# Nine of the eleven input slots of each attention layer as seven block products

## What is computed

```python
for l in range(DEPTH):                      # DEPTH = 2
    h = rmsnorm(x, attn_norm[l])            # [256, 1024]
    proj = h @ w_in[l]                      # q_a, kv_a, g_a, q_b, k_b, v_b, uv_c
    q_a, kv_a, g_a, q_b, k_b, v_b, uv_c = jnp.split(proj, IN_OFFSETS, axis=-1)
    ... # rope on q_a, k_slc, k_win, q_b, k_b; three attention branches; chunked_sgu on uv_c
    x = x + mixed @ w_out[l]
    h = rmsnorm(x, ffn_norm[l])
    x = x + (jax.nn.silu(h @ w_ffn1[l]) * (h @ w_ffn3[l])) @ w_ffn2[l]
```

## Time and profile before

| | |
|---|---|
| median of 3 runs | 2492.07 us (2491.85 to 2494.61) |
| the profiled execution | 2493.16 us, of which the span of the trace is 2491.4 us |
| TensorE busy | 2404.8 us, 97% of the span |
| VectorE, ScalarE, GpSimd busy | 903.9, 366.1 and 68.6 us |
| mean granted TensorE clock | 0.99 |

### The profile page before, as it was taken

One profiled execution on the slowest core, in us unless ns is written; L12 is line 12 of the kernel. 1 busy time (PEld: TensorE's weight loads), 2 busy tenths in 40 slices (PEclk: granted clock), 3 DMA queues, 4 the chain that ended last, 5 costly groups with the idle time before them and its releaser, 6 DMA issues.

```text
span 2491.4 us, 78654 instructions
## 1 busy us (share of the span) xinstructions
PE 2404.8 (97%) x35626; PEld 2107.3 (85%) x35626; DVE 903.9 (36%) x1881; ACT 366.1 (15%) x818; POOL 68.6 (3%) x134
## 2 busy tenths in 40 slices
PE   8899999999999999999999899999999999999997
PEld 7788787899999999999999788788877887788885
DVE  1367776421010101101010222433777323334676
ACT  1211112300000000000000112410111123401111
POOL 5000000000000000000000000000000000000000
PEclk9999999999999999999999999999999999999999
DMA  7255454599999999999999645234555553245551
GB/s 229 80 174 170 168 186 136 197 369 394 380 387 395 394 395 394 395 395 394 395 394 395 205 138 170 94 110 135 170 170 168 157 160 120 86 135 161 170 168 68
DMA packets 347708, 585.23 MB, mean 235 GB/s; under 512 B 13508, under 2 KB 187784, under 8 KB 347608
## 3 DMA queue, kind: packets, MB, share of 16 engines
q1 hardware_dynamic: 341400, 581.00, 66.0%
q10 hardware_dynamic: 5728, 2.27, 0.4%
q0 software_dynamic: 480, 0.50, 0.2%
HBM read 582.69 MB, written 1.05 MB: 234 GB/s over the span
## 4 chain that ended last, share of the span: by engine, by line
PE 85%; DMA 10%; ACT 2%; DVE 2%; issue 1%; POOL 0%; ACTq 0%; SPq 0%; DVEq 0%; POOLq 0%
PE ps L787 16%; PE ps L928 16%; PE ps L656 14%; PE ps L800 8%; PE ps L646 8%; PE ps L943 7%; DMA weight_ring<-in_moe_w_gate 5%; DMA weight_ring<-in_moe_w_up 4%; PE ps L738 4%; PE ps L695 2%; PE ps L688 2%; PE ps L991 1%; PE ps L638 1%; DVE x_res L1749 1%; PE ps L954 1%
## 5 line engine op out<-in xcount | busy, mean ns | idle before, releaser
L928 PE MATMUL ps<-heads_feat,weight_ring 128*64 128x84 f32 x14336 | 542.2, 237 | 9.0 <-DMA weight_ring<-in_moe_w_gate 5.3
L928 PEld LDWEIGHTS ps<-heads_feat,weight_ring 128*64 128x64 f32 x14336 | 526.1, 137 | 21.3 <-issue 15.3
L943 PE MATMUL ps<-scores,weight_ring 128*64 128x84 f32 x7168 | 276.2, 237 | 2.8
L943 PEld LDWEIGHTS ps<-scores,weight_ring 128*64 128x64 f32 x7168 | 265.2, 137 | 10.6 <-issue 10.6
L656 PE MATMUL ps<-h_feat,weight_ring 128*128 128x256 f32 x1152 | 261.4, 387 | 2.1 <-ACT probs_feat L1371 2.0
L656 PEld LDWEIGHTS ps<-h_feat,weight_ring 128*128 128x128 f32 x1152 | 220.8, 193 | 36.4 <-issue 4.9
L1749 DVE SCALAR_TENSOR_TENSOR gelu_tmp<-gelu_tmp,ps 128x336 f32<-128x336 f32 (+1 forms) x59 | 30.3, 514 | 524.2 <-ACT gelu_tmp L1445 519.3
L787 PE MATMUL ps<-proj 128*64 128x128 f32 x3168 | 195.4, 273 | 0.0
L646 PE MATMUL ps<-weight_ring,h_feat 128*128 128x256 f32 x864 | 187.9, 379 | 0.6 <-ACT heads_feat L1371 0.6
L646 PEld LDWEIGHTS ps<-weight_ring,h_feat 128*128 128x128 f32 x864 | 163.8, 190 | 23.1 <-issue 1.0
L787 PEld LDWEIGHTS ps<-proj 128*64 128x64 f32 x3168 | 177.5, 137 | 0.0
(11 more groups left out here) (310 smaller groups left out, 2394.9 us busy)
## 6 DMA issues: line engine op xcount, KB each, us to landing
weight_ring<-in_moe_w_gate SPq DMA_DIRECT2D x112, 1024.0 KB, 10.8
weight_ring<-in_moe_w_down SPq DMA_DIRECT2D x112, 1024.0 KB, 11.5
weight_ring<-in_moe_w_up SPq DMA_DIRECT2D x104, 1024.0 KB, 11.3
weight_ring<-in_w_ffn SPq DMA_DIRECT2D x66, 1024.0 KB, 5.3
weight_ring<-in_w_in SPq DMA_DIRECT2D x30, 1024.0 KB, 5.3
weight_ring<-in_w_merge SPq DMA_DIRECT2D x24, 1024.0 KB, 5.3
weight_ring<-in_ffn_w_gate SPq DMA_DIRECT2D x14, 1024.0 KB, 5.0
weight_ring<-in_ffn_w_up SPq DMA_DIRECT2D x14, 1024.0 KB, 5.0
```

The lines of the kernel that those rows point to most:

```text
L928: mm = pe.matmul(out_[c:c + 64], w[:, k, m * P + c:m * P + c + 64], hcur[:, 4 * j + k, :], start=(j == 0 and m % each == 0 and k == 0), st ...
L943: mm = pe.matmul(ps[c:c + 64, 4 + d // 4, (d % 4) * CAP:(d % 4 + 1) * CAP], w[:, f, d * P + c:d * P + c + 64], HBS[:, 2 * j + f, :], start ...
```

## The change: what it does

For c = 2 to 10 of both layers (n = 0 to 8 here, "slot n"), TensorE runs `single` in place of `act_job(token_major(...))`: seven block products per slot. Products 0 to 2 need the weights as they landed and the token sums `HS1` (`in_tokens_summed`); products 3 to 5 wait for `singles_summed`, three weight sums that VectorE makes in `single_sums`; product 6 waits for `singles_differed`, one difference that GpSimd makes in `differences`. Results go to PSUM banks 4 and 5 or 6 and 7 in turn, ScalarE copies them to `PR1` in `heads_feat`, VectorE adds them up into `proj` (`single_out`). The sums lie in `merge_gates`. VectorE's stream takes the new work in between the rope groups: `inputs_to(c)` does `single_out(n)` and then `single_sums(n + 2)` for all slots up to c. TensorE's transposes of heads wait also for `singles_combined`.

```diff
@@ job_starts
-        act += [(f"in{l}", 12), (f"pos{l}", 1), ...
+        act += [(f"in{l}", 3), (f"pos{l}", 1), ...
@@ views
+        WS1 = [SG[:, i * 2048:(i + 1) * 2048].rearrange("p (m k n) -> p m k n", m=4, k=4) for i in range(2)]
+        HS1 = SG[:, 4096:6144].rearrange("p (m k n) -> p m k n", m=4, k=4)
+        PR1 = [TT[:, i * 1536:(i + 1) * 1536] for i in range(2)]
@@ gpsimd, called behind the second norm power of each layer's first norm
+            def differences(l):
+                pool.wait_ge(sem("in_tokens_summed"), l + 1)
+                for c in range(2, 11):
+                    n, q = 9 * l + c - 2, SLOT[f"in{l}"] + c
+                    pool.wait_ge(sem(f"slot_in{q % SLOTS}"), 16 * (q // SLOTS + 1))
+                    pool.wait_ge(sem("slots_used"), q - 1)
+                    w = w_slot(q).rearrange("p (j k i n) -> p j k i n", j=2, k=4, i=2)
+                    pool.tensor_tensor(WS1[n % 2][:, 2, :, :], w[:, 0, :, 0, :], w[:, 0, :, 1, :],
+                                       ALU.subtract).then_inc(sem("singles_differed"), 1)
@@ tensor
+            def single(n, by_token):
+                w = slot().rearrange("p (j k i n) -> p j k i n", j=2, k=4, i=2)
+                ws = WS1[n % 2]
+                if n >= 2:
+                    pe.wait_ge(sem("singles_copied"), 2 * (n - 1))
+                for m, (a, b) in enumerate((
+                        (w[:, 0, :, 0, :], hT[:, 0:4, 0:P]), (w[:, 1, :, 0, :], hT[:, 4:8, 0:P]),
+                        (w[:, 1, :, 1, :], HS1[:, 3, :, :]), (ws[:, 0, :, :], HS1[:, 0, :, :]),
+                        (ws[:, 1, :, :], HS1[:, 1, :, :]), (ws[:, 3, :, :], hT[:, 4:8, P:2 * P]),
+                        (ws[:, 2, :, :], HS1[:, 2, :, :]))):
+                    if m == 3:
+                        pe.wait_ge(sem("singles_summed"), n + 1)
+                    if m == 6:
+                        pe.wait_ge(sem("singles_differed"), n + 1)
+                    out_ = ps[:, 4 + 2 * (n % 2) + m // 4, m % 4 * P:(m % 4 + 1) * P]
+                    lhs, rhs = (b, a) if by_token else (a, b)
+                    for k in range(4):
+                        for c in (0, 64):
+                            mm = pe.matmul(out_[c:c + 64], lhs[:, k, c:c + 64], rhs[:, k, :], ...)
+                    if m == 3:
+                        mm.then_inc(sem("singles_half_full"), 1)
+                mm.then_inc(sem("slots_used"), 1)
...
+                pe.wait_ge(sem("in_tokens_summed"), l + 1)
                 for c in range(2, 11):
-                    w = slot().rearrange("p (k n) -> p k n", k=KT)
-                    act_job(token_major(h_tok, w), True)
+                    single(9 * l + c - 2, True)
...
                 pe.wait_ge(sem("dup_ready"), 2 * (l + 1))
+                pe.wait_ge(sem("singles_combined"), 9 * (l + 1))
@@ scalar
+                def single(n, q):
+                    if n >= 2:
+                        act.wait_ge(sem("singles_combined"), n - 1)
+                    act.wait_ge(sem("singles_half_full"), n + 1)
+                    copy(PR1[n % 2][:, 0:512], ps[:, 4 + 2 * (n % 2), :]).then_inc(sem("singles_copied"), 1)
+                    act.wait_ge(sem("slots_used"), q + 1)
+                    copy(PR1[n % 2][:, 512:896], ps[:, 5 + 2 * (n % 2), 0:384]).then_inc(sem("singles_copied"), 1)
-                for c in range(11):
+                for c in range(2):
                     inputs(c, SLOT[f"in{l}"] + c)
+                for c in range(2, 11):
+                    single(9 * l + c - 2, SLOT[f"in{l}"] + c)
@@ vector
+            def single_sums(n, q):
+                dve.wait_ge(sem(f"slot_in{q % SLOTS}"), 16 * (q // SLOTS + 1))
+                w = w_slot(q).rearrange("p (j k i n) -> p j k i n", j=2, k=4, i=2)
+                ws = WS1[n % 2]
+                link(tt(ws[:, 0, :, :], w[:, 0, :, 1, :], w[:, 1, :, 1, :], ALU.add))
+                link(tt(ws[:, 1, :, :], ws[:, 0, :, :], w[:, 0, :, 0, :], ALU.subtract))
+                tt(ws[:, 3, :, :], w[:, 1, :, 0, :], ws[:, 1, :, :], ALU.subtract).then_inc(sem("singles_summed"), 1)
+            def single_out(n, o):
+                dve.wait_ge(sem("singles_copied"), 2 * n + 2)
+                ...
+                link(tt(pr[:, 7, :], pr[:, 0, :], pr[:, 4, :], ALU.add))
+                link(tt(pr[:, 8:10, :], pr[:, 7:8, :].to_broadcast([P, 2, P]), by_three[:, 1:3, :], ALU.add))
+                tt(o[:, :, 0, :], by_three[:, 0:4:3, :], pr[:, 1:3, :], ALU.add)
+                tt(o[:, :, 1, :], pr[:, 8:9, :].to_broadcast([P, 2, P]), pr[:, 5:7, :], ALU.add).then_inc(
+                    sem("singles_combined"), 1)
@@ vector, layer loop
                 norm(at["attn_norm_2"] + 8 * l, second, None, ahead, behind)
+                token_sums(HS1, "in_tokens_summed")
+                for c in (2, 3):
+                    single_sums(9 * l + c - 2, SLOT[f"in{l}"] + c)
+                done = [2]
+                def inputs_to(c):
+                    while done[0] <= c:
+                        d = done[0]
+                        single_out(9 * l + d - 2, PJ2[...])
+                        if d + 2 < 11:
+                            single_sums(9 * l + d, SLOT[f"in{l}"] + d + 2)
+                        done[0] += 1
+                    dve.wait_ge(sem("singles_combined"), 9 * l + c - 1)
...
-                    dve.wait_ge(sem("act_drained"), JOB[f"in{l}"] + (c0 + HD * nh - 1) // COLS + 1)
+                    if n == 0:
+                        dve.wait_ge(sem("act_drained"), JOB[f"in{l}"] + 2)
+                    else:
+                        inputs_to((c0 + HD * nh - 1) // COLS)
...
+                inputs_to(10)
```

More of the change, by code:

```diff
@@ L594, in _ @@
                 turn(name)
+                for l in range(L2):
+                    if i == norm_powers[9 + 4 * l]:
+                        differences(l)
         @block.tensor
@@ L717, in start_stage @@
                 n_act[0] += 2
+            def single(n, by_token):
[16 more added lines that the diff above has]
+                        for c in (0, 64):
+                            mm = pe.matmul(out_[c:c + 64], lhs[:, k, c:c + 64], rhs[:, k, :],
+                                           start=(m % 4 == 0 and k == 0), stop=(k == 3), skip_group_check=True)
+                    if m == 3:
+                        mm.then_inc(sem("singles_half_full"), 1)
+                mm.then_inc(sem("slots_used"), 1)
             def out_stage(lhs, by_feature=False):
@@ L1809, in _, with token_sums @@
             steps_done, outs_done, seven_done, calls = [0], [0], [0], [0]
-            def token_sums():
+            def token_sums(hs=HS, name="tokens_summed"):
                 dve.wait_ge(sem("dve_drained"), n_job[0])
                 h = hT[:, :, :].rearrange("p (j k) (l n) -> p j k l n", j=2, l=2)
[L1815 to L1818, removed]
+                link(tt(hs[:, 0, :, :], h[:, 0, :, 1, :], h[:, 0, :, 0, :], ALU.subtract))
+                link(tt(hs[:, 1, :, :], h[:, 1, :, 1, :], hs[:, 0, :, :], ALU.subtract))
+                tt(hs[:, 2, :, :], h[:, 1, :, 1, :], h[:, 0, :, 1, :], ALU.subtract)
+                tt(hs[:, 3, :, :], h[:, 1, :, 0, :], hs[:, 1, :, :], ALU.subtract).then_inc(sem(name), 1)
+            def single_sums(n, q):
[7 more added lines that the diff above has]
+                dve.wait_ge(sem("singles_copied"), 2 * n + 2)
+                pr = PR1[n % 2].rearrange("p (a n) -> p a n", n=P)
+                by_three = PR1[n % 2].rearrange("p (a n) -> p a n", n=3 * P)[:, :, 0:P]
+                link(tt(pr[:, 7, :], pr[:, 0, :], pr[:, 4, :], ALU.add))
[3 more added lines that the diff above has]
+                    sem("singles_combined"), 1)
             def weight_sums(b, q, rounds, z):
@@ L2339, in _ @@
                 norm(at["attn_norm_2"] + 8 * l, second, None, ahead, behind)
+                token_sums(HS1, "in_tokens_summed")
[5 more added lines that the diff above has]
+                        d = done[0]
+                        single_out(9 * l + d - 2, PJ2[:, :, d * COLS:(d + 1) * COLS].rearrange("p t (i n) -> p i t n", i=2))
+                        if d + 2 < 11:
+                            single_sums(9 * l + d, SLOT[f"in{l}"] + d + 2)
+                        done[0] += 1
+                    dve.wait_ge(sem("singles_combined"), 9 * l + c - 1)
                 link(tt(GT[:, 0:128].rearrange("p (a d) -> p a d", a=2), lv[:, 0:4:2, :], lv[:, 1:4:2, :], ALU.mult))
```

2 lines of the change are left out of this document (1 added, 1 removed).

## The result

The changed kernel takes 2479.08 us (median of 5 runs, 2477.76 to 2481.93), before 2492.25; the ratio is 0.9946, 95% interval 0.9932 to 0.9961. It is 13.2 us faster. Timed again later beside other kernels it took 2479.57 us (5 runs, ratio 0.9941, 0.9927 to 0.9955); the ten runs together have a median of 2479.3. The forecast was 2483.8, 4.7 us above the measured time: the sign and the mechanism were right, the gain was forecast too small. The profiled execution has a span of 2476.2 us and took 2477.97.

The account below looks back on a forecast made before the run. TensorE was taken to bound the kernel: 2493.16 profiled - 12.9 gain + 2 x 2.2 GpSimd loss + 2 x 0.1 stage end = 2484.9, less 1.1 for the median of runs, 2483.8 us; range 2478.8 to 2491.

Parts of the forecast that it names:

- TensorE's gain: Nine slots per layer, input stage: 6.19 us per slot instead of 6.91, 0.72 less, 12.9 us for 18 slots.
- The loss to GpSimd: Input stage: GpSimd's differences hold VectorE up, so TensorE waits at slots 2, 5 and 7, 2.2 us per layer.
- the walk: Input stage: VectorE's queue priced in order against TensorE's wants; slack about 3 us without exclusion, 2.2 us lost per layer with it.
- The price p: Length of one GpSimd difference, 1.15 us, middle of 0.525 and 1.78; VectorE assumed to stand still for all of it.
- VectorE's own work: Queue in the input stage: three weight sums 2.1 us and four additions 1.6 us per slot, 0.03 us per link included.
- Forecast lateness at slot 7: VectorE's sums for slot 7 ready at 48.1 us, wanted at 46.8: 1.3 late, after 0.6 and 0.1 before.
- VectorE's operation at 14.49: Trace near 15 us: VectorE operation of 0.82 us overlapped by a GpSimd one, taken as evidence that they hold each other up.
- Start and end of the stage: Input stage: start costs nothing; last additions end at 58.0 us, transposes come at 58.2; 0.1 us per layer charged.
- T: Time in us from where TensorE begins slot 0 of a layer; first rope group forecast at about +4.2.
- Nothing is lost to GpSimd: Rival, input stage: ports not shared or differences near the fill's 0.525 us, so no waits; 2479.4 us, chance 0.30.
- The waits halve TensorE's clock: Rival: one clock fall per layer after waits, 2487.7 us; chance 0.20, shared with p of 1.3 to 1.6.
- VectorE becomes the bound: Rival, input stage: differences of 2.3 us make each layer wait 10.9 us; 2501.2 us, slower than before; chance 0.10.

Follow-up runs that it names:

- fills: Changed kernel with GpSimd's weight difference replaced by four zero fills of the same buffer per slot; 2479.32 us, ratio 0.9943.
- the small products first: Changed kernel with VectorE's small products for lam_arg queued ahead of the token sums; 2478.41 us in a single execution, then 2479.25 us, ratio 0.9936.
- the two kernels that wait longest: Changed kernel with each GpSimd difference made twice, 2491.23 us, and changed kernel with the third weight sum made twice, GpSimd's difference kept, 2493.68 us.
- two differences: Changed kernel with GpSimd making each weight difference twice, one behind the other; 2491.23 us, ratio to before 0.9998.
- one more sum: Changed kernel with VectorE making each slot's third weight sum twice, GpSimd's difference kept; 2493.68 us, ratio 1.0001.
- the repetition: The unmodified changed kernel timed and profiled a second time beside other kernels; 2479.57 us, ratio 0.9941.
- VectorE's difference: Changed kernel with the weight difference made by VectorE instead of GpSimd, 2481.30 us; with the small products for lam_arg also moved first, 2481.17 us.

## Why the prediction was right and where it was wrong

**TensorE's gain** was mis-sized, and too small: 0.717 us per slot predicted, 0.795 found (6.91 less 6.113), 14.3 us for 18 slots and 14.0 in the chain. The row was read rightly but holds more than products: in the feed-forward part slots in pairs stand between other matmuls, and 12.38 us are 14 products of 0.873, 12.22, and 0.16 around them. Inside a run of nine slots that comes about once. That is 1.1 us of the miss.

**The loss to GpSimd** is the step that failed: "2.2 us per layer" in waits at slots 2, 5 and 7, the largest part of the miss of 4.7 us. It was 0.0 and 0.36 us in one profiled execution, 0.36 and 0.36 in the other, at slot 2 alone, so 0.4 to 0.7 in all where 4.4 were forecast. The mechanism was right: VectorE does stand still for a part of each difference, it doesn't for fills, and with load added the waits came at slots 2, 5 and 7. Two sizes in the walk were off, each by little, and the walk adds them up. *The price p*: 1.15 us forecast, 0.83 to 0.98 measured for the seven differences that hit VectorE in layer 0 between its first rope group and the sums of slot 7, together 1.5 us less. (The forecast took the middle of two bounds for the length of a difference and let VectorE lose all of it; the length is 1.27 us, nearer to the prediction's other estimate of 1.35, and the loss is less than the length.) *VectorE's own work*: 3.7 us per slot forecast, 3.5 measured (sums 2.05, additions 1.47), because the price of a link was charged to operations that depend on nothing just before them, and these start 0.61 us apart and not 0.72; 1.1 us by slot 7. Against that the faster slots ask 0.5 us sooner. Forecast lateness at slot 7 was 2.0 (with what was late at 2 and 5), less 2.6, plus 0.5: 0.1 us early; measured 0.3 early in layer 0 and 0.2 in layer 1. The stage runs at the edge of its slack, so errors of 5 to 20% in the prices turned into the whole loss.

The ground for the loss was thinner than the prediction says. VectorE's operation at 14.49 has one large input and not two, so that row is of another kind than the operations of the stage, and only GpSimd is seen to lose time in it. Nor do the operations at 1944.05 prepare the rope, as the prediction calls them: they are the last of the norm; nothing hangs on that.

**Start and end of the stage** came as forecast: no wait at the start, and the transposes of heads start 2.54 us behind the gate product's start instead of 2.46, 0.1 us per layer as charged. ScalarE's first copy came later than forecast, and with it the first rope group, at T = +5.2 and +5.6 instead of +4.2. That is why slot 2 and not slot 7 is where TensorE waits: with the small products first the group starts at +0.8, the sums of slot 2 are 3.7 us ahead and those of slot 7 hardly move.

**The rivals.** "Nothing is lost to GpSimd" gave 2479.4, which is what the clock says, but for a reason that is false. Its number came true by luck: the slack covered the loss, and the 0.4 to 0.7 us of waits that it had at nothing stood against 1.1 us of gain that it lacked. "The waits halve TensorE's clock" did not happen in the changed kernel, whose granted clock is 1.00 in all nine slots, but is real: the two kernels that wait longest have four falls within the slots. "VectorE becomes the bound" was far off with p near 1, yet two differences, or one more sum, are enough to give back the whole gain.

**The sum again** with what the traces show: 2493.16 - 14.0 + 0.4 + 0.2 - 1.1 = 2478.7 with the profile's waits, 2479.0 with the repetition's 0.7; measured 2479.1 and 2479.6.

## What to carry to other kernels

Where work is moved from the engine that bounds to one beside it, walk the second engine's queue up to each time that its results are wanted, with start-to-start distances of the operations read from a timeline, dependent and independent apart; the answer is a slack per place, and an error in a price is multiplied by the number of operations ahead of it. A loss to another engine that shows in the durations costs nothing until that slack is used up: read the longest of a group, not its mean or median, then test with a little load added. When one operation can stand on either engine, count for GpSimd what it takes from VectorE: here mostly 0.94 to 1.08 us for an operation that VectorE itself does in 0.6 to 0.7. That paid only under added load. In the kernel as it is the operation on VectorE brought nothing: the two kernels that have it there have a median of 2481.2 us over ten runs, the changed kernel 2479.3, and whether these 2 us are the kernel's or those of single executions is open.

## What the runs showed that was not expected

*A fall of TensorE's clock cost 1.7 us wherever TensorE had its products in a row.* In the run of two differences the products behind the waits lose 1.72 us at slot 5 of layer 0 and 1.71 at slot 7 of layer 1, in the run of one more sum 1.7 behind the waits at slot 7. The length of the single wait does not decide it: 2.6 and 2.2 us at slots 2 and 5 of layer 1 brought none, 2.2 us at slot 7 in the other kernel did. Where TensorE waits between its products anyway, as between the transposes of heads, such a fall cost only 0.8 us.

*The same step goes far to explain how executions differ.* The changed kernel was timed again to see how far a median of five runs holds:

> The changed kernel itself, timed again beside the others. Theory (its executions spread over 4 us because single falls of the granted clock of about 1.7 us each come in other stages, and two medians of five runs differ by up to 2 us for that): a median between 2478 and 2481. Rival (the kernel with VectorE's difference, at 2481.2 and 2481.3 in two calls, is really 2 us slower than the changed one): 2479.1 within 0.5 us again.

It came to 2479.57 (2478.76 to 2481.46), inside the theory's bounds and also within the rival's half microsecond, so this run by itself decides nothing. The profiles say more. From the end of layer 0's slots to the first product of layer 1's lie 480.0 us in the profile of two differences, 481.1 with one more sum, 482.7 in the changed kernel, 484.4 with VectorE's difference: nearly equal steps, for 0.5 of the 480.0 is a wait at the heads that only this run has. The windows of 8 us in the attention part between lose 0.0, 1.8, 3.4 and 5.0 us of clock, that is none, one, two and three falls. The window with the most in it, of one more sum, of the changed kernel and of VectorE's difference:

```profile
1520.00:1528.00 8.00, 8.00 (x36) 6.83 (x35) 6.84 (x11) 2.62 (x3) 0.00 (x0) 0.81 0.02 5
```

```profile
1512.00:1520.00 8.00, 8.00 (x26) 6.65 (x27) 6.94 (x11) 2.54 (x2) 0.00 (x0) 0.69 0.00 0
```

```profile
1512.00:1520.00 8.00, 8.00 (x29) 6.56 (x28) 6.90 (x11) 2.54 (x2) 0.00 (x0) 0.62 0.01 4
```

A clock of 0.79 over 8 us is 1.7 us lost. So single executions with equal slots come to stand some microseconds apart, and smaller differences were read from the stage and not from the times. That the medians of five runs, up to 2 us apart, differ for this reason alone fits but is not shown: one execution of each kernel was profiled. Whether a kernel can make such falls rarer was not tried.
